# Local attention in a streaming encoder block: 64 queries on their own 128 keys instead of 128 queries on 192 keys

## The chip, the cores and the metric

The kernel runs on one NeuronCore of one Trainium2 chip. The metric is the device time of one execution in microseconds (us). Engines are named as the profile names them: PE is TensorE (PEld its weight loads), DVE is VectorE, ACT is ScalarE, POOL is GpSimd, SP issues the DMAs. Everything is computed in fp32. An ordinary fp32 matrix product stands in the trace as two loads of weights and two MATMUL records (a pair of records per product); a transpose stands as one of each. The large products use fp32r operands that the kernel has split into a high and a low part, three products for one.

## What is computed

One block on 2048 tokens of width 1024: an input projection, a sliding-window attention (the part that the change touches), a pooling branch, a cross-attention into 256 memory tokens, three sigmoid gates, an output product, an MLP of width 4096 and a final norm. The window attention has 8 query heads in 2 groups of 4 that share keys and values (head dimension 64). A query in chunk n (chunks of 64 tokens) sees all keys of chunks n-1 and n, that is 128 keys, with a bias of minus slope times distance and a sink logit per head:

```python
def _window_attention(q, k, v, sinks):
    ...
    qb = q.reshape(b, nc, CHUNK, N_KV_HEADS, Q_PER_KV, HEAD_DIM)
    kb = _chunk_band(k, nc)
    vb = _chunk_band(v, nc)
    scores = jnp.einsum('bnqgrd,bnkgd->bngrqk', qb, kb).astype(jnp.float32) * (HEAD_DIM ** -0.5)
    ...
    scores = scores - slopes * dist[None, :, None, None]
    scores = jnp.where(valid[None, :, None, None], scores, NEG_INF)
    ...
    probs = jax.nn.softmax(jnp.concatenate([scores, sink], axis=-1), axis=-1)[..., :-1]
    out = jnp.einsum('bngrqk,bnkgd->bnqgrd', probs.astype(v.dtype), vb)
```

## The kernel before

The sequence is worked in four blocks of 512 tokens (`NBLK`), one turn of a hardware loop on every engine. A block has these stages in order: input projection (keys, values, queries), four window-attention steps `i` = 0 to 3 of 128 queries each, four memory-attention steps with the first gate and the attention branch's product, merge, output product, MLP, final norm. Weights come in pieces of 1024 by 256: SP loads a piece into one of two `stage` slots, ACT copies the high part to `w_hi` (`hi(n, ...)`), DVE subtracts for `w_lo` (`lo(n)`), PE multiplies (`piece(...)`, two tiles of eight k-steps of three products, L979 to L981). Outputs go through a ring of PSUM banks 0 to 3; the attention uses banks 4 to 7 (`ATT` = 4).

The order on each engine is written out by hand. In one window step `i` PE does, in this order:

- the scores of 128 queries, L1077. A query tile of 128 tokens covers two chunks, so it is multiplied with 192 keys (`WIN_KEYS`). The weights (stationary operand) are one head's 128 queries on 64 partitions, the moving operand is the keys. Heads 0 to 3 sit on partitions 0 to 63, heads 4 to 7 on partitions 64 to 127. A PSUM bank holds 512 columns, so the eight heads' parts are packed by the table `SCORE_PARTS` into three banks: ten products, of 192, 128 or 64 keys. Bank 6 takes parts of both halves, and the semaphore `rest_done` keeps the second half's from starting before the first half's is done.
- `piece(W_U + i, ...)`: 48 large products. Between them, at the fifth and the sixth k-step of the second tile (`probs_across`), the probabilities are transposed: per half of the heads four transposes of keys 0 to 127 and four of keys 128 to 191, L984.
- the value products, L1108 and L1109: per head one product on the first 128 keys and one that adds the last 64 keys, each with 64 weight columns (the head dimension). Even heads write PSUM partitions 0 to 63, odd heads partitions 64 to 127, all in bank 7.

Meanwhile DVE adds the distance bias to the scores (L700, one instruction for each part, slope times `dist`), takes the maximum (L705) and forms the exponent's bias (L706 to L708) for each half `f` of four heads, then sums and reciprocals (L716, L717) and scales the probabilities (L718), then splits the next weight piece (`lo(n + 1)`, L611). ACT splits the next piece (`hi(n + 1)`), does the exponentials per head, copies the transposed probabilities out of PSUM (`pt_a`, `pt_b`) and the value product's result into `y0_hi`; DVE writes `y0_lo` (L724). All of ACT's operations stand at L351. PE waits for DVE before the transposes (`p_rdy`) and for ACT before the value products (`pt_rdy`).

At the start of a block PE transposes the values of 576 tokens in tiles of 128 (`v_tm`, five transposes of `v_pad`), and ACT copies the queries into `q_att`, one head pair for each tile.

Of the kernel before, what the change touches and what calls it, by code (L numbers as in the profile page):

```python
# [31 lines left out]
WIN_KEYS = 3 * CHUNK  # L32
# [24 lines left out]


REST = [[(4 * g + 3, 0, WIN_KEYS, 2, g * 256), (4 * g + 2, P, CHUNK, 2, g * 256 + WIN_KEYS)] for g in range(NKV)]
SCORE_PARTS = REST[0] + [(4 * g + r, 0, WIN_KEYS if r < 2 else P, g, r * WIN_KEYS) for g in range(NKV) for r in range(3)] \  # L60
    + REST[1]

# [23 lines left out]
def build(nc, a, out):  # L86
# [27 lines left out]
    q_att = at("q_att", [P, 4, TB], F32, arena + 16 * KB)  # L114
    resid = at("resid", [P, KT, TB], F32, arena + 16 * KB)
    scores = at("scores", [P, NQ, WIN_KEYS], F32, arena + 32 * KB)
    pt_a = at("pt_a", [P, NQ, P], F32, arena + 38 * KB)
    pt_b = at("pt_b", [HD, NQ, P], F32, arena + 42 * KB)
# [27 lines left out]
    v_tm = sb("v_tm", [P, TT + 1, P])  # L146
    dist0 = sb("dist0", [P, WIN_KEYS])
    dist = sb("dist", [P, WIN_KEYS])
# [4 lines left out]
    half_bg = sb("half_bg", [P, 24])  # L153
    sink = sb("sink", [P, NQ])
# [42 lines left out]
    rest_done = sem("rest_done")  # L197
# [47 lines left out]
    w_upv, w_downv, w_mkv = kp(a["w_up"][0]), kp(a["w_down"][0]), kp(a["w_mem_kv"][0])  # L245
    w_br = [kp(a[n][0]) for n in ("w_branch_attn", "w_branch_pool", "w_branch_mem")]
# [8 lines left out]
    def by_head(t, slot, tile, paired):  # L255


        if paired:
            return t[:, slot, :, tile * P:(tile + 1) * P].rearrange("p k (g c) -> p k g c", g=NKV)
        return t[:, slot, :, :].rearrange("p k (g c) -> p k g c", g=NKV)[:, :, :, tile * HD:(tile + 1) * HD]  # L260

    block = nc.Block()
    with block:
# [3 lines left out]
        def _(sp):  # L267
# [17 lines left out]
            for n in range(PIECES0):  # L285
                load(n % 2, w_mkv[:, :, n * PC:(n + 1) * PC], n - 1 if n >= 2 else None)
                if n == 1:
                    sp.dma_start(x_tm[:], x_rows[:, 0:TT, :]).then_inc(x_ld, 16)
                    sp.dma_start(sink[:], a["attn_sinks"][0:1, :].broadcast_to([P, NQ])).then_inc(const_ld, 16)
                    sp.dma_start(g_fin[:], a["norm_final_g"].rearrange("(o n) -> o n", o=1).broadcast_to([P, D]))\  # L290
                        .then_inc(const_ld, 16)
# [6 lines left out]
            with sp.Fori(0, NBLK) as b:  # L298
# [50 lines left out]
        def _(act):  # L349
# [63 lines left out]
            with act.Fori(0, NBLK) as b:  # L413
# [23 lines left out]
                for t in range(4):  # L437
                    if t == 2:
                        hi(W_U, G_Q + 2)
                    copy(q_att[:, t, :], G_Q + t)  # L440
                copy(v_tm[:, 0:TT, :].rearrange("p t n -> p (t n)"), G_VT)
                copy(v_tm[0:CHUNK, TT, :], G_VT + 1, ring[0:CHUNK, (G_VT + 1) % 4, 0:P])


                for i in range(TT):
# [19 lines left out]
                    if i == 0:  # L465

                        act.wait_ge(stored, b + 1)
                    op(y0_hi[:, :, i * P:(i + 1) * P], ps[:, ATT + 3, :].rearrange("p (t n) -> p t n", n=P),
                       ACT.Copy).then_inc(y_hi_done, 1)
# [130 lines left out]
        def _(dve):  # L600
            v = nc.vector

            def low(slot, value, kt=KT, query=False):
# [12 lines left out]
            v.scalar_tensor_tensor(out=dist[:], in0=dist0[:], scalar=-1.0, in1=dist0[:], op0=ALU.mult, op1=ALU.max)\  # L616
                .then_inc(d, 1)
# [3 lines left out]
            v.reciprocal(inv_cnt[:], inv_cnt[:]).then_inc(fin_done, 1)  # L621

            v.memset(dist[0:CHUNK, 2 * CHUNK:], FAR).then_inc(y_done, 1)
            v.memset(dist[CHUNK:P, 0:CHUNK], FAR).then_inc(d, 1)
            dve.wait_ge(d, 6)
            v.tensor_copy(dist0[:], dist[:]).then_inc(d, 1)
            dve.wait_ge(d, 7)

            v.memset(dist0[0:CHUNK, 0:CHUNK], FAR).then_inc(d, 1)
# [32 lines left out]
            dve.wait_ge(const_ld, 32)  # L662
            v.tensor_scalar(sink8[:], sink[:], 1.0 / ATT_SCALE, None, ALU.mult).then_inc(d, 1)
# [3 lines left out]
            d0 = 15  # L667

            D_BLK = 59
            with dve.Fori(0, NBLK) as b:  # L670
# [20 lines left out]
                for i in range(TT):  # L691
# [3 lines left out]
                    dst_ = dist0 if i == 0 else dist  # L695
# [13 lines left out]
                    if i == 0:  # L709

                        v.tensor_copy(dist0[:], dist[:]).then_inc(d, 1)
                        step[0] += 1
                    for f in range(2):
# [10 lines left out]
                    v.tensor_tensor(y0_lo[:, :, i * P:(i + 1) * P],  # L724
                                    ps[:, ATT + 3, :].rearrange("p (t n) -> p t n", n=P),
                                    y0_hi[:, :, i * P:(i + 1) * P].bitcast(F32), ALU.subtract).then_inc(y_done, 1)
# [166 lines left out]
        def _(pool):  # L893
# [8 lines left out]
            g_.iota(dist0[:], [[-1, WIN_KEYS]], base=CHUNK, channel_multiplier=1,  # L902
# [71 lines left out]
        def _(pe):  # L974
# [50 lines left out]
            with pe.Fori(0, NBLK) as b:  # L1025
# [33 lines left out]
                for t in range(TT):  # L1059
                    last = transpose(ring[:, G_VT % 4, t * P:(t + 1) * P], v_pad[:, t * P:(t + 1) * P])  # L1060
                last.then_inc(tile_done, 1)
                transpose(ring[0:CHUNK, G_VT % 4 + 1, 0:P], v_pad[:, TB:TB + CHUNK]).then_inc(tile_done, 1)

                for i in range(TT):
# [18 lines left out]
                    def probs_across(k):  # L1083
# [181 lines left out]
```

## Time and profile before

| what | value |
|---|---|
| median of 3 runs | 3052.1 us (3051.82 to 3055.05) |
| profiled execution: span | 3050.7 us |
| PE busy | 3000.1 us (98%) |
| DVE busy | 1367.5 us (45%) |
| ACT busy | 982.3 us (32%) |
| POOL busy | 194.1 us (6%) |
| granted TensorE clock, mean | 0.996 of 2.4 GHz |
| HBM traffic | 96 GB/s over the span |

The profiled execution's span is 1.4 us below the median of the runs. Matmul records overlap in the trace: a record lasts longer than the time until the next one starts, so what a group of products costs is read from the starts of what comes first and what comes next, and not from its busy time. Rows of the timeline give the start in us, the duration, the engine, the line, the operation, its operands and shape, how many were merged, and in brackets the idle time before and what ended it.

### The profile page before, as it was taken

The numbers are of one execution on the slowest core, as the hardware profiler recorded it, in microseconds if no ns is written. First come the engines' busy times: TensorE is split into PE (matmuls) and PEld (weight loads), VectorE is DVE, ScalarE is ACT, GpSimd is POOL, SyncE is SP. The second block draws the span as 40 slices with busy tenths as digits, with TensorE's granted clock in tenths as the row PEclk, the third lists the DMA queues.
The fourth block names the chain that finished last, engine by engine and source line by source line (L and its number), as shares of the span: only waits on it lengthen the run. The fifth ranks groups of instructions, "written<-read, shape, count | busy, mean of one in ns | idle before, by whom it ended". The sixth has DMA issues, their size and how long they took to land.

```text
span 3050.7 us, 36914 instructions
## 1 busy us (share of the span) xinstructions
PE 3000.1 (98%) x14045; PEld 2468.1 (81%) x14045; DVE 1367.5 (45%) x1709; ACT 982.3 (32%) x1457; POOL 194.1 (6%) x191
## 2 busy tenths in 40 slices
PE   8999999999999999999999999999999999999998
PEld 7788888888778888888877888888887788888886
DVE  4542354444344335544435424544444532454444
ACT  4442232222344233222234423322223432332223
POOL 0100110000010111000001011100000101100000
PEclk9999999999999999999999999999999999999999
DMA  5122333322312233333231224233322122432322
GB/s 187 35 78 85 118 131 97 97 96 97 98 39 90 90 124 118 97 97 100 93 98 39 83 90 164 84 102 97 97 91 84 51 82 97 160 97 92 98 97 86
DMA packets 290351, 294.06 MB, mean 96 GB/s; under 512 B 9704, under 2 KB 285212, under 8 KB 290204
## 3 DMA queue, kind: packets, MB, share of 16 engines
q1 hardware_dynamic: 287900, 283.71, 28.8%
q0 software_dynamic: 2304, 8.39, 0.7%
q8 instruction: 92, 1.51, 0.2%
q14 instruction: 55, 0.45, 0.0%
HBM read 283.67 MB, written 8.39 MB: 96 GB/s over the span
## 4 chain that ended last, share of the span: by engine, by line
PE 90%; issue 5%; DVE 2%; POOL 1%; ACT 1%; DMA 0%; POOLq 0%; DVEq 0%; ACTq 0%
PE ps L979 28%; PE ps L981 27%; PE ps L980 27%; PE ps L984 2%; PE ps L1108 2%; PE ps L1109 2%; PE ps L1077 1%; POOL sq_sum L957 1%; PE ps L1135 1%; PE ps L1118 1%; ACT sq L351 0%; DVE u_lo L792 0%; DVE scores L700 0%; DVE mx L705 0%; DVE out_tm L883 0%
## 5 line engine op out<-in xcount | busy, mean ns | idle before, releaser
L979 PE MATMUL ps<-h_hi,w_hi 128*128 128x512 f32 x2240 | 884.8, 395 | 12.5 <-issue 12.5
L980 PE MATMUL ps<-h_lo,w_hi 128*128 128x512 f32 x2240 | 874.6, 390 | 0.0
L981 PE MATMUL ps<-h_hi,w_lo 128*128 128x512 f32 x2240 | 874.6, 390 | 0.0
L611 DVE TENSOR_TENSOR w_lo<-stage,w_hi 128x2048 fp32r<-128x2048 f32 (+1 forms) x269 | 559.9, 2081 | 643.2 <-ACT w_hi L351 642.0
L351 ACT ACTIVATE w_hi<-stage 128x2048 fp32r<-128x2048 f32 (+2 forms) x287 | 485.1, 1693 | 525.7 <-PE ps L981 524.5
L979 PE MATMUL ps<-u_hi,w_hi 128*128 128x512 f32 x1280 | 501.5, 392 | 5.5 <-DVE u_lo L792 5.5
L979 PEld LDWEIGHTS ps<-h_hi,w_hi 128*128 128x128 f32 x2240 | 422.1, 188 | 100.6 <-issue 14.2
L981 PE MATMUL ps<-u_hi,w_lo 128*128 128x512 f32 x1280 | 498.8, 390 | 0.0
L980 PE MATMUL ps<-u_lo,w_hi 128*128 128x512 f32 x1280 | 498.4, 389 | 0.0
L981 PEld LDWEIGHTS ps<-h_hi,w_lo 128*128 128x128 f32 x2240 | 421.9, 188 | 88.1
L980 PEld LDWEIGHTS ps<-h_lo,w_hi 128*128 128x128 f32 x2240 | 422.1, 188 | 86.4 <-issue 1.0
L979 PEld LDWEIGHTS ps<-u_hi,w_hi 128*128 128x128 f32 x1280 | 240.4, 188 | 56.9 <-DVE u_lo L792 4.4
L981 PEld LDWEIGHTS ps<-u_hi,w_lo 128*128 128x128 f32 x1280 | 240.3, 188 | 50.2
L980 PEld LDWEIGHTS ps<-u_lo,w_hi 128*128 128x128 f32 x1280 | 240.5, 188 | 48.8
L351 ACT ACTIVATE u_hi<-temp 128x512 fp32r<-128x512 f32 x128 | 80.9, 632 | 512.3 <-DVE temp L836 512.3
L854 DVE TENSOR_TENSOR resid<-resid,ps 128x512 f32<-128x512 f32 x128 | 88.0, 688 | 338.0 <-PE ps L981 338.0
L351 ACT ACTIVATE temp<-ps,half_bg 128x512 f32<-128x512 f32 x96 | 66.1, 689 | 357.8 <-PE ps L981 357.8
L836 DVE SCALAR_TENSOR_TENSOR temp<-ps,inv_rms 128x512 f32<-128x512 f32 x128 | 88.5, 692 | 205.3 <-PE ps L981 204.8
L979 PE MATMUL ps<-y_hi,w_hi 128*128 128x512 f32 x400 | 157.6, 394 | 0.0
L981 PE MATMUL ps<-y_hi,w_lo 128*128 128x512 f32 x400 | 155.9, 390 | 0.0
L980 PE MATMUL ps<-y_lo,w_hi 128*128 128x512 f32 x400 | 155.8, 389 | 0.0
L949 POOL TENSOR_TENSOR resid<-resid,temp 128x512 f32<-128x512 f32 x64 | 83.9, 1321 | 938.0 <-DVE temp L784 938.0
(154 smaller groups left out, 2081.9 us busy)
## 6 DMA issues: line engine op xcount, KB each, us to landing
stage<-in_w_up SPq DMA_DIRECT2D x128, 512.0 KB, 4.6
stage<-in_w_down SPq DMA_DIRECT2D x128, 512.0 KB, 4.0
stage<-in_w_gate SPq DMA_DIRECT2D x96, 512.0 KB, 4.2
stage<-in_w_in SPq DMA_DIRECT2D x60, 512.0 KB, 4.7
stage<-in_w_out SPq DMA_DIRECT2D x32, 512.0 KB, 4.1
x_tm<-in_x SPq DMA_DIRECT2D x5, 2048.0 KB, 9.5
stage<-in_w_branch_attn SPq DMA_DIRECT2D x32, 256.0 KB, 3.0
stage<-in_w_branch_pool SPq DMA_DIRECT2D x32, 256.0 KB, 3.0
```

What stands on the lines that cost most here:

```text
L351: return nc.scalar.activation(*args, **kw)
L611: v.tensor_tensor(w_lo[:, slot, 0:kt, :], stage[:, slot, 0:kt, :], w_hi[:, slot, 0:kt, :].bitcast(F32), ALU.subtract).then_inc(lo_done, 1)
L836: v.scalar_tensor_tensor(out=temp[:, t % 2, :], in0=ring[:, t % 4, :], scalar=0.0, in1=inv_rms[:], op0=ALU.max, op1=ALU.mult)\
L854: v.tensor_tensor(resid[:, 2 * i + z, :], resid[:, 2 * i + z, :], ring[:, t % 4, :], ALU.add).then_inc(emptied[t % 4], 1)
L949: g_.tensor_tensor(dst, dst, temp[:, 2 * g + z, :], ALU.add).then_inc(sum_rdy, 1)
L957: g_.tensor_tensor(sq_sum[:], sq_sum[:], sq[:, m % 2, :], ALU.add).then_inc(sq_add, 1)
L979: mm(dst, wh, xh, start=first, stop=False)
L980: mm(dst, wh, xl, start=False, stop=False)
L981: return mm(dst, wl, xh, start=False, stop=last)
L984: return nc.tensor.transpose(dst, src, ident[0:n, 0:n])
L1108: mm(o, v_tm[:, i, g * HD:(g + 1) * HD], pt_a[:, h, :], start=True, stop=False)
L1109: last = mm(o, v_tm[0:HD, i + 1, g * HD:(g + 1) * HD], pt_b[:, h, :], start=False, stop=True)
```

## The change

A score tile now holds two heads of one chunk (2 by 64 queries) instead of one head of two chunks, and meets only the 128 keys which its chunk may see.

- `q_att` is laid out by chunk, `[P, chunk, pair member, 64]`, so that two heads of a chunk are 128 adjacent columns. A step `i` has eight score products of 128 keys (2 chunks, 2 head pairs, 2 groups), with the groups, and so the partition halves, alternating. Group 0 writes bank 4 and group 1 bank 5 alone; `rest_done` is gone.
- The bias is precomputed for each head pair (`bias`, and `bias0` for the first chunk, whose keys before it are masked by -1e30). DVE adds it with two TENSOR_TENSOR of 256 columns for each half in place of five SCALAR_TENSOR_TENSOR.
- Maximum, exponential and scaling work on 128 instead of 192 columns for each of the eight tiles.
- There is one transpose for each tile (eight in a step, sixteen before), two copies `pt` by ACT (four before).
- The value product takes the transposed probabilities of two tiles, four heads, as one moving operand of 256 columns: four products of 64 weight columns in a step (sixteen before). Group 0 writes PSUM partitions 0 to 63, group 1 partitions 64 to 127.
- `v_tm` holds the 128 keys of each of the eight chunks, overlapping: eight transposes and two copies of 512 columns at a block's start, before five transposes and copies of 512 and 128 columns.
- The channel order of `y0` changes with this, so `w_branch_attn` is loaded to match: two DMAs of 64 partitions by 4 rows, before two of 128 partitions by 2 rows, of the same 128 KB each.
- The sinks are rearranged by four small copies at the start, and the bias tables are built at the start: eight operations of 64 by 128 and a few more. `dist` and `v_tm` move into the shared arena. In step 0 of a block `bias0` is overwritten with `bias`, 512 columns (before `dist0`, 192 columns).

```diff
-WIN_KEYS = 3 * CHUNK
+WIN_KEYS = 2 * CHUNK
+NCH = TB // CHUNK
...
                     load(n % 2, w_gate[:, :, j * PC:(j + 1) * PC], lo0 + n)
-                    load((n + 1) % 2, w_br[0][:, :, j * PC:(j + 1) * PC], lo0 + (n + 1), kt=4)
+                    load((n + 1) % 2, [w_attn[g][:, :, j * PC:(j + 1) * PC] for g in range(NKV)], lo0 + (n + 1),
+                         dst=[stage[g * HD:(g + 1) * HD, (n + 1) % 2, 0:4, :] for g in range(NKV)])
...
-                    copy(q_att[:, t, :], G_Q + t)
-                copy(v_tm[:, 0:TT, :].rearrange("p t n -> p (t n)"), G_VT)
-                copy(v_tm[0:CHUNK, TT, :], G_VT + 1, ring[0:CHUNK, (G_VT + 1) % 4, 0:P])
+                    copy(q_att[:, :, t, :], G_Q + t, ring[:, (G_Q + t) % 4, :].rearrange("p (c n) -> p c n", n=CHUNK))
+                for z in range(2):
+                    copy(v_tm[:, 4 * z:4 * z + 4, :].rearrange("p t n -> p (t n)"), G_VT + z)
...
-                        op(pt_a[:, hs, :].rearrange("p h n -> p (h n)"), ps[:, ATT + f, :], ACT.Copy)
-                        last = op(pt_b[:, hs, :].rearrange("p h n -> p (h n)"), ps[0:HD, ATT + 2 + f, :], ACT.Copy)
+                        last = op(pt[:, hs, :].rearrange("p h n -> p (h n)"), ps[:, ATT + f, :], ACT.Copy)
...
-                        for h, k0, n_, bank, col in SCORE_PARTS:
-                            if h // HALF == f:
-                                last = v.scalar_tensor_tensor(
-                                    out=scores[:, h, k0:k0 + n_], in0=dst_[:, k0:k0 + n_],
-                                    scalar=-SLOPES[h] / ATT_SCALE, in1=ps[:, ATT + bank, col:col + n_],
-                                    op0=ALU.mult, op1=ALU.add)
+                        for c in range(2):
+                            last = v.tensor_tensor(scores[:, f * HALF + 2 * c:f * HALF + 2 * c + 2, :],
+                                                   (bias if c else first)[:, 2 * f:2 * f + 2, :],
+                                                   ps[:, ATT + f, c * 256:(c + 1) * 256].rearrange("p (t n) -> p t n", t=2),
+                                                   ALU.add)
...
-                    for h, k0, n_, bank, col in SCORE_PARTS:
-                        g, t = h // 4, h % 4
-                        if (h, k0, n_, bank, col) == REST[1][0]:
-
-
-                            pe.wait_ge(rest_done, b4 + (i + 1))
-                        last = mm(ps[:, ATT + bank, col:col + n_], q_att[g * HD:(g + 1) * HD, t, i * P:(i + 1) * P],
-                                  k_pad[g * HD:(g + 1) * HD, i * P + k0:i * P + k0 + n_], start=True, stop=True)
-                        if (h, k0, n_, bank, col) == REST[0][1]:
-                            last.then_inc(rest_done, 1)
+                    for c in range(2):
+                        for t in range(2):
+                            for g in range(NKV):
+                                last = mm(ps[:, ATT + g, (2 * c + t) * P:(2 * c + t + 1) * P],
+                                          q_att[g * HD:(g + 1) * HD, 2 * i + c, 2 * t:2 * t + 2, :].rearrange("p t n -> p (t n)"),
+                                          k_pad[g * HD:(g + 1) * HD, (2 * i + c) * CHUNK:(2 * i + c) * CHUNK + P],
+                                          start=True, stop=True)
...
                         for h in range(f * HALF, (f + 1) * HALF):
-                            transpose(ps[:, ATT + h // 4, (h % 4) * P:(h % 4 + 1) * P], scores[:, h, 0:P])
-                        for h in range(f * HALF, (f + 1) * HALF):
-                            last = transpose(ps[0:HD, ATT + 2 + h // 4, (h % 4) * P:(h % 4 + 1) * P],
-                                             scores[:, h, P:])
+                            last = transpose(ps[:, ATT + f, (h % HALF) * P:(h % HALF + 1) * P], scores[:, h, :])
...
-                    for h in range(NQ):
-                        g = h // 4
-                        o = ps[(h % 2) * HD:(h % 2 + 1) * HD, ATT + 3, (h // 2) * P:(h // 2 + 1) * P]
-                        mm(o, v_tm[:, i, g * HD:(g + 1) * HD], pt_a[:, h, :], start=True, stop=False)
-                        last = mm(o, v_tm[0:HD, i + 1, g * HD:(g + 1) * HD], pt_b[:, h, :], start=False, stop=True)
+                    for c in range(2):
+                        for g in range(NKV):
+                            last = mm(ps[g * HD:(g + 1) * HD, ATT + 3, c * 256:(c + 1) * 256],
+                                      v_tm[:, 2 * i + c, g * HD:(g + 1) * HD],
+                                      pt[:, 4 * g + 2 * c:4 * g + 2 * c + 2, :].rearrange("p t n -> p (t n)"),
+                                      start=True, stop=True)
```

On PE, the scores at a block's first step, before; `k_pad` are the keys, `q_att` the queries, shapes are output rows by columns:

```order
L1077 MATMUL ps<-k_pad,q_att 128x192
L1077 MATMUL ps<-k_pad,q_att 128x64
L1077 MATMUL ps<-k_pad,q_att 128x192 x2
L1077 MATMUL ps<-k_pad,q_att 128x128
L1077 MATMUL ps<-k_pad,q_att 128x192 x2
L1077 MATMUL ps<-k_pad,q_att 128x128
L1077 MATMUL ps<-k_pad,q_att 128x192
L1077 MATMUL ps<-k_pad,q_att 128x64
```

and on PE from the first half's transposes of the same step to the next step's scores, now (`pt` are the transposed probabilities, `v_tm` the values):

```order
L998 MATMUL ps<-ident,scores 128x128 x4
L993 MATMUL ps<-h_hi,w_hi 128x512
L994 MATMUL ps<-h_lo,w_hi 128x512
L995 MATMUL ps<-h_hi,w_lo 128x512
...
L1116 MATMUL ps<-pt,v_tm 64x256 x4
L1089 MATMUL ps<-k_pad,q_att 128x128 x8
```

The ten score products of three widths have become eight of 128 columns, and the value products between the last large product and the next scores are four of 256 columns, where before eight rows of L1108 and eight of L1109, in turn and of 128 columns, stood.

On DVE, one half's bias and maximum in the first step, before:

```order
L700 SCALAR_TENSOR_TENSOR scores<-dist_89,ps 128x192
L700 SCALAR_TENSOR_TENSOR scores<-dist_89,ps 128x64
L700 SCALAR_TENSOR_TENSOR scores<-dist_89,ps 128x192 x2
L700 SCALAR_TENSOR_TENSOR scores<-dist_89,ps 128x128
...
L705 TENSOR_REDUCE mx<-scores 128x4
```

and now:

```order
L715 TENSOR_TENSOR scores<-bias_89,ps 128x256
L715 TENSOR_TENSOR scores<-bias,ps 128x256
...
L720 TENSOR_REDUCE mx<-scores 128x4
```

Two additions stand where five multiply-adds stood; nothing else has changed its place on DVE inside the step.

## Rows read from the trace of the kernel before

**Rows 1.** The page: busy time of the engines, and the chain that ended last.

```profile
PE 3000.1 (98%) x14045; PEld 2468.1 (81%) x14045; DVE 1367.5 (45%) x1709; ACT 982.3 (32%) x1457; POOL 194.1 (6%) x191
...
PE 90%; issue 5%; DVE 2%; POOL 1%; ACT 1%; DMA 0%; POOLq 0%; DVEq 0%; ACTq 0%
```

**Rows 2.** Waits of PE: who waited for whom, total us, times, longest.

```profile
PE ps L1077 <- ACT q_att L351: 1.3, 4, 0.3
PE ps L984 <- DVE scores L718: 1.1, 4, 0.3
```

**Rows 3.** Timeline of PE, second block: start us, us, what, xcount, [idle before].

```profile
826.52 0.71 PE L984 MATMUL ps<-ident,v_pad 128*128 128x128 f32 x5
827.57 2.61 PE L1077 MATMUL ps<-k_pad,q_att 64*128 64x192 f32 x20 [0.34 <-ACT q_att L351]
...
830.11 0.50 PE L979 MATMUL ps<-h_hi,w_hi 128*128 128x512 f32 x1
...
838.39 1.03 PE L984 MATMUL ps<-ident,scores 128*128 128x128 f32 x8
...
839.95 1.03 PE L984 MATMUL ps<-ident,scores 128*128 128x128 f32 x8
...
842.98 0.43 PE L1108 MATMUL ps<-pt_a,v_tm 128*64 128x128 f32 x2
843.35 0.43 PE L1109 MATMUL ps<-pt_b,v_tm 64*64 64x128 f32 x2
...
848.76 2.61 PE L1077 MATMUL ps<-k_pad,q_att 64*128 64x192 f32 x20
...
851.30 0.50 PE L979 MATMUL ps<-h_hi,w_hi 128*128 128x512 f32 x1
```

**Rows 4.** Timeline of other fp32 products of the block, PE and its weight loads.

```profile
931.99 1.95 PE L1135 MATMUL ps<-m_pt,mem_v 128*128 128x128 f32 x16
...
912.89 1.59 PEld L1118 LDWEIGHTS ps<-mem_k,q_mem 128*128 128x128 f32 x8 [0.17 <-issue]
```

**Rows 5.** Timeline of score weight loads alive at 828.20, 828.70 and 829.60 us.

```profile
828.11 0.30 PEld L1077 LDWEIGHTS ps<-k_pad,q_att 64*128 64x128 f32 x2
...
828.55 0.35 PEld L1077 LDWEIGHTS ps<-k_pad,q_att 64*128 64x128 f32 x4
...
829.42 0.30 PEld L1077 LDWEIGHTS ps<-k_pad,q_att 64*128 64x128 f32 x2
```

**Rows 6.** Groups of PEld by form: busy us, mean ns, idle before and why.

```profile
L1108 PEld LDWEIGHTS ps<-pt_a,v_tm 128*64 128x64 f32 x256 | 24.5, 134 | 24.8 <-issue 24.8
```

**Rows 7.** Timeline of DVE in a window step.

```profile
830.22 1.21 DVE L700 SCALAR_TENSOR_TENSOR scores<-dist,ps 128x192 f32<-128x192 f32 x5 [9.66 <-PE ps L1077]
831.47 0.95 DVE L705 TENSOR_REDUCE mx<-scores 128x4 f32<-128x768 f32 x1
...
835.64 0.25 DVE L711 COPY dist<-dist 128x192 f32<-128x192 f32 x1
...
838.17 0.96 DVE L718 TENSOR_TENSOR scores<-scores,rd 128x768 f32<-128x768 f32 x1
839.04 2.29 DVE L611 TENSOR_TENSOR w_lo<-stage,w_hi 128x2048 fp32r<-128x2048 f32 x1
849.49 0.69 DVE L724 TENSOR_TENSOR y_lo<-ps,y_hi 128x512 fp32r<-128x512 f32 x1 [8.16 <-ACT y_hi L351]
```

**Rows 8.** Timeline of ACT, a window step's last copy and a branch piece's split.

```profile
841.52 0.58 ACT L351 ACTIVATE pt_b<-ps 64x512 f32<-64x512 f32 x1
...
937.30 1.05 ACT L351 ACTIVATE w_hi<-stage 128x1024 fp32r<-128x1024 f32 x1
```

**Rows 9.** Timeline of SP and DMA issues (KB each, median us to landing), 890 to 930 us.

```profile
927.83 0.88 SPq L283 DMA_DIRECT2D stage<-in_w_branch_attn  x2
...
stage<-in_w_branch_attn SPq DMA_DIRECT2D x2, 256.0 KB, 2.9
```

**Rows 10.** Timeline of DVE at the program's start.

```profile
7.35 0.21 DVE L631 COPY par<-ps 128x52 f32<-128x52 f32 x1 [3.17 <-PE ps L984]
...
40.35 2.29 DVE L611 TENSOR_TENSOR w_lo<-stage,w_hi 128x2048 fp32r<-128x2048 f32 x1 [2.81 <-ACT w_hi L351]
```

More of the change, by code:

```diff
@@ L145, in build @@
     v_pad = sb("v_pad", [P, CHUNK + TB])
-    v_tm = sb("v_tm", [P, TT + 1, P])
-    dist0 = sb("dist0", [P, WIN_KEYS])
-    dist = sb("dist", [P, WIN_KEYS])
+    v_tm = at("v_tm", [P, NCH, P], F32, arena + 42 * KB)
+    dist = at("dist", [P, WIN_KEYS], F32, arena + 40 * KB)
+    bias0 = sb("bias0", [P, 4, WIN_KEYS])
+    bias = sb("bias", [P, 4, WIN_KEYS])
     g_fin = sb("g_fin", [P, D])
@@ L260, in by_head, with y0_tile, by_chunk @@
         return t[:, slot, :, :].rearrange("p k (g c) -> p k g c", g=NKV)[:, :, :, tile * HD:(tile + 1) * HD]
+    def y0_tile(t, i):
+        return t[:, :, i * P:(i + 1) * P].rearrange("p t (c n) -> p c t n", c=2)
+    def by_chunk(bank):
+        return bank.rearrange("p (c t n) -> p c t n", c=2, t=4)
     block = nc.Block()
@@ L467, in _ @@
                         act.wait_ge(stored, b + 1)
-                    op(y0_hi[:, :, i * P:(i + 1) * P], ps[:, ATT + 3, :].rearrange("p (t n) -> p t n", n=P),
-                       ACT.Copy).then_inc(y_hi_done, 1)
+                    op(y0_tile(y0_hi, i), by_chunk(ps[:, ATT + 3, :]), ACT.Copy).then_inc(y_hi_done, 1)
                 for j in range(4):
@@ L621, in _ @@
             v.reciprocal(inv_cnt[:], inv_cnt[:]).then_inc(fin_done, 1)
-            v.memset(dist[0:CHUNK, 2 * CHUNK:], FAR).then_inc(y_done, 1)
-            v.memset(dist[CHUNK:P, 0:CHUNK], FAR).then_inc(d, 1)
+            v.scalar_tensor_tensor(out=bias[:, 0, :], in0=dist[:], scalar=-1.0, in1=dist[:], op0=ALU.mult, op1=ALU.max)\
+                .then_inc(y_done, 1)
+            dve.wait_ge(y_done, 1)
+            v.tensor_copy(dist[:], bias[:, 0, :]).then_inc(d, 1)
             dve.wait_ge(d, 6)
-            v.tensor_copy(dist0[:], dist[:]).then_inc(d, 1)
+            for c in range(4):
+                for r in range(2):
+                    rows_ = slice(r * CHUNK, (r + 1) * CHUNK)
+                    last = v.tensor_scalar(bias[rows_, c, :], dist[rows_, :], -SLOPES[2 * c + r] / ATT_SCALE, None, ALU.mult)
+            last.then_inc(d, 1)
             dve.wait_ge(d, 7)
-            v.memset(dist0[0:CHUNK, 0:CHUNK], FAR).then_inc(d, 1)
+            v.tensor_copy(bias0[:, :, CHUNK:], bias[:, :, CHUNK:])
+            v.memset(bias0[:, :, 0:CHUNK], -FAR).then_inc(d, 1)
             dve.wait_ge(misc_done, 1)
@@ L662, in _ @@
             dve.wait_ge(const_ld, 32)
+            for r in range(2):
+                rows_ = slice(r * CHUNK, (r + 1) * CHUNK)
+                by_pair = sink_h[rows_, :].rearrange("p (g t r) -> p g t r", g=NKV, t=2)[:, :, :, r]
+                for c in range(2):
+                    last = v.tensor_copy(sink[rows_, :].rearrange("p (g c t) -> p g c t", g=NKV, c=2)[:, :, c, :], by_pair)
+            last.then_inc(d, 1)
+            dve.wait_ge(d, 14)
             v.tensor_scalar(sink8[:], sink[:], 1.0 / ATT_SCALE, None, ALU.mult).then_inc(d, 1)
@@ L666, in _ @@
             low(1, 6, query=True)
-            d0 = 15
+            d0 = 16
             D_BLK = 59
@@ L694, in _ @@
                     dve.wait_ge(att_done, att0 + (4 * i + 1))
-                    dst_ = dist0 if i == 0 else dist
+                    first = bias0 if i == 0 else bias
                     for f in range(2):
                         hs = slice(f * HALF, (f + 1) * HALF)
-                        for h, k0, n_, bank, col in SCORE_PARTS:
-                            if h // HALF == f:
-                                last = v.scalar_tensor_tensor(
-                                    out=scores[:, h, k0:k0 + n_], in0=dst_[:, k0:k0 + n_],
-                                    scalar=-SLOPES[h] / ATT_SCALE, in1=ps[:, ATT + bank, col:col + n_],
-                                    op0=ALU.mult, op1=ALU.add)
+                        for c in range(2):
[3 more added lines that the diff above has]
+                                                   ALU.add)
                         chained(last)
@@ L709, in _ @@
                     if i == 0:
-                        v.tensor_copy(dist0[:], dist[:]).then_inc(d, 1)
+                        v.tensor_copy(bias0[:], bias[:]).then_inc(d, 1)
                         step[0] += 1
@@ L1058, in _ @@
                     pe.wait_ge(emptied[G_VT % 4 + z], e0 + G_VT // 4)
[L1059 to L1062, printed above, removed]
+                for z in range(2):
+                    for t in range(4):
+                        c = 4 * z + t
+                        last = transpose(ring[:, G_VT % 4 + z, t * P:(t + 1) * P], v_pad[:, c * CHUNK:c * CHUNK + P])
+                    last.then_inc(tile_done, 1)
                 for i in range(TT):
@@ L1104, in _ @@
                             pe.wait_ge(emptied[G_VT % 4 + z], e0 + (G_VT // 4 + 1))
-                    for h in range(NQ):
-                        g = h // 4
-                        o = ps[(h % 2) * HD:(h % 2 + 1) * HD, ATT + 3, (h // 2) * P:(h // 2 + 1) * P]
-                        mm(o, v_tm[:, i, g * HD:(g + 1) * HD], pt_a[:, h, :], start=True, stop=False)
-                        last = mm(o, v_tm[0:HD, i + 1, g * HD:(g + 1) * HD], pt_b[:, h, :], start=False, stop=True)
+                    for c in range(2):
+                        for g in range(NKV):
[3 more added lines that the diff above has]
+                                      start=True, stop=True)
                     last.then_inc(att_done, 1)
```

23 lines of the change are left out of this document (9 added, 14 removed).

## The prediction

> **What bounds the kernel now.** The page's busy times come first: PE is busy for 98% of the span, and the chain that ended last runs through PE for 90% [rows 1]. So the question is how much PE time the window attention takes, and whether another engine becomes late when PE gets faster. Next come the waits of PE: in all 16 window steps PE lost 1.1 us to late probabilities and, at the four block starts, 1.3 us to late queries [rows 2]. The attention steps are thus PE's own work, and that work is read from starts in PE's timeline [rows 3]. In the second block the scores start at 827.57 and the next large product at 830.11: 2.54 us. The value products start at 842.98, the next scores at 848.76: 5.78 us. Eight transposes last 1.03 us as merged, their last record alone about 0.27, so one follows another after (1.03 - 0.27) / 7 = 0.109 us; sixteen are 1.74 us. A step costs PE 2.54 + 5.78 + 1.74 = 10.06 us beside its large products, and 16 steps 161 us. The clock is at its upper level (2.4 GHz) in these stretches; the page's mean of 0.996 leaves nothing to win there.
>
> **Unit prices.** Sixteen records of 128 columns follow each other after (1.95 - 0.28) / 15 = 0.11 us. The eight weight loads between products of 256 columns follow after (1.59 - 0.19 - 0.11) / 6 = 0.215 us; the 0.11 is the first gap, in which the array has not yet begun [rows 4]. So a record costs 0.11 at 128 columns and 0.215 at 256, two to a product. The ten score products carry 1536 columns, at 0.215 for 256 and two records 2.58 us of streaming alone, and yet they take 2.54 us with their filling and emptying. Part of it overlapped, and the loads show where: at 828.20 and 829.60 two loads are alive, 0.30 us from the first start to the last end; at 828.70 four are alive within 0.35 us, so that three gaps fill 0.35 - 0.19 = 0.16 us, 0.05 each, half of what one product after another allows [rows 5]. That is the place where the products of heads 0 to 3 (partitions 0 to 63) hand over to those of heads 4 to 7. Two partition halves work at the same time. The value products show the contrary: L1108 starts at 842.98, L1109 at 843.35, a step of 0.36 us where two records of 128 columns need 0.22 [rows 3], and the weight load before each stands idle for 24.8 / 128 = 0.19 us [rows 6]. Each of the sixteen products begins only when the one before has left the array. Each also changes between 128 and 64 contracted rows.
>
> **Transposes.** Eight instead of sixteen: 8 x 0.109 = 0.87 us saved a step. At a block's start three are added, 0.33 us. Before, the five start at 826.52, the last ends its streaming some 0.5 us after, and the scores begin only at 827.57, held by the copy of the last queries [rows 3]. The 0.33 fits in these 0.5 us and costs nothing; without that cover it would be 4 x 0.33 = 1.3 us.
>
> **Scores.** Eight products of 128 columns, sixteen records, with the halves alternating and each in its own bank. If both halves run at once, each has eight records: 0.11 to load, 7 x 0.11 to the last start, 0.20 from the last start to the next large product (before, the group ends at 827.57 + 2.61 = 830.18, its last record of 0.27 began at 829.91, the next product at 830.11), together 1.08, and about 0.12 lag of the second half: 1.2 us. If they run one after another: 0.11 + 15 x 0.11 + 0.20 = 2.0 us. I take 1.2, since the trace shows the overlap with the very same operands, and saved are 1.34 us a step.
>
> **Value products.** Four of 64 weight columns and 256 moving columns. All contract 128 rows; nothing changes between them but the half of the output partitions. Lower bound, both halves of columns at once: 0.05 us (half a load) + 0.215 to the second record, 2 x 0.215 to the last start, 0.31 to the next group (0.20 plus the 0.11 by which the record is longer), 1.0, with a lag 1.1 us. In between, one after another without emptying: 0.27 + 6 x 0.215 + 0.31 = 1.9 us. Upper bound, each product waits as today: four times 0.36 + 2 x (0.215 - 0.11) = 0.57, that is 2.3 us. No row shows two column halves with equal rows in a row of products, so all three stay possible. I take 1.1: a mere change of the half did not empty the array where the trace has one [rows 5], and what all the slow products share is the changing number of rows, which is gone. Saved: 5.78 - 1.1 = 4.68 us a step.
>
> Two rules of the Trainium skill bear on this place, and they pull apart. The page "TensorEngine Tiling (Array Packing)", Tiling Modes, Key Properties, says that a change of the tiling mode drains the array, a change of the tile alone does not, and that tiles can load and multiply in parallel; the 0.36 us of rows 3 and the loads of rows 5 agree, and no row shows it for column tiles. The page "TensorE: Matmul & The Clock Gate", Part 3, says that a weight load overlaps a running matmul only where the row group differs; the four value products all use every row. By the first the step costs 1.1 us, by the second near 2.3.
>
> **What lies beside PE.** The chain from scores to probabilities gets shorter. Today DVE starts at 830.22 and ends the second scaling at 838.17 + 0.96 = 839.13, 8.9 us later, with five additions (1.21), a maximum (0.95) and a scaling (0.96) for each half [rows 7]. Two additions of 256 columns are bounded by 2 x 0.69 (512 columns, L724) and 1.21 x 512 / 768 = 0.8; I take 0.8. Maximum and scaling at two thirds of the columns are 0.65 each. A half saves about 0.4 + 0.3 + 0.3, the chain some 2 us after both halves and the smaller exponentials. The overwriting of `bias0` in a block's first step grows from 0.25 to at most 0.25 x 512 / 192 = 0.67. From scores to transposes PE still has its own 8 us of large products (830.11 to 838.39, [rows 3]). One thing comes later: `y0_lo` (0.69 after its wait) must leave DVE before the next scores, and with scores of 1.2 us it ends some 0.2 us after them; the 2 us cover that. So the wait for late probabilities vanishes, 1.1 us in all [rows 2]. ACT's last copy of probabilities ended at 841.52 + 0.58 = 842.10, 0.9 us before the values [rows 8, 3]; the transposes of the second half are now 0.43 us shorter, but so are the copies, one instead of two. DVE's next piece (`lo`, 2.29) ends at 841.33 and is wanted at 851.30; a step shrinks by 7 us, the chain before it by 2, so about 5 us remain. The branch weights come by 64 partitions instead of 128: issued at 927.83, landing 2.9 us later, split at 937.30, that is 6.5 us of cover [rows 8, 9]; even twice the transfer time hides. The start: DVE stands idle 3.17 us before `par`, and the new bias operations (some fifteen, each of 128 columns or fewer by partition, mostly 0.1 to 0.3) fit; the sink copies fall into 2.81 us [rows 10]. These edits cost nothing; uncovered, the start would cost up to 2 us once.
>
> **The sum.** 1.34 + 4.68 + 0.87 = 6.89 us a step, 16 steps 110.2, plus 1.1: 111 us. From the profiled span 3050.7 that leaves 2939.4; the median of the runs lies 1.4 above the span, so I predict **2941 us**.
>
> **Rivals.**
> - Columns one after another: the value products take 1.9, that is 16 x 0.8 = 13 us more, 2954 us. For it: twice the operand stream on the same 128 partitions at once has no row in the trace.
> - Columns emptied at each product: 16 x 1.2 = 19 us more, 2960 us. For it: the sixteen products of today, which also alternate halves. Against: they always change the row number too. This is the second page's rule.
> - Rows one after another: the overlap of rows 5 lasts only over a handover, and alternating might lose it. Scores 2.0, 13 us more: 2954 with fast columns, 2973 with emptied ones.
> - A new wait takes the place: PE arrives at the transposes before the probabilities. For that the DVE chain would have to lose the 2 us that it gains. At 1 us late a step that is 16 us, 2957 us.
> - Slower than before: the same wait, if the new additions and scalings (three-dimensional operands over half-tiles) ran much slower than the rows of the same size. PE gains 6.9 us a step and has about 2 to spare, so the chain must grow by 9 us, from 7 to 16, before the kernel is slower; at 18 us it is 16 x 2 = 32 us over, 3084 us. Nothing in rows 7 points to it.
> - The edit does not do what it says: the two halves of a score tile need no less PE time. Excluded by the count of columns, 1536 to 1024.
>
> **How the numbers follow.** Forecast 50%; columns in turn 18%; columns emptied 14%; rows in turn with any columns 10%; a wait for DVE of up to 2 us a step 5%; slower 2%; more gain than forecast (no lags: 16 x 0.2 = 3 us, 2938) 1%. The range from 2935 to 2962 holds the first three and part of the others. Faster by over 0.2% (what a measurement here can tell from no change) 0.97, within 0.2% 0.01, slower 0.02.
>
> **What would show it.** Right: score group to next large product 1.2 us, values to next scores 1.1, weight loads of scores and of values alive four at a time, no PE wait for the scaling on DVE (L718). Wrong: gaps of 0.2 us before each value load mean emptied columns; record starts spaced 0.215 without gaps mean columns in turn; a PE wait for DVE scores in each step means the chain.

## The result and the profile after

| | before | changed |
|---|---|---|
| median of the runs | 3052.3 us (4 runs) | 2946.24 us (2944.52 to 2946.61, 4 runs) |
| span of the profiled execution | 3050.7 us | 2944.8 us |
| ratio, with its 95% interval | | 0.9647 (0.9634 to 0.9661) |

The forecast was 2941 us in a range from 2935 to 2962. The changed kernel is 106 us faster, 3.5%, where 111 were forecast. The page of the changed kernel opens like that of before [rows 1]: PE is still busy for 98% of a span that is 106 us shorter.

```profile
PE 2890.6 (98%) x13481; PEld 2391.0 (81%) x13481; DVE 1350.5 (46%) x1625; ACT 961.5 (33%) x1425; POOL 195.3 (7%) x191
...
PE 90%; issue 5%; DVE 2%; POOL 1%; ACT 1%; DMA 0%; DVEq 0%; POOLq 0%; ACTq 0%
```

The changed kernel's PE in the second block, transposes of the values, scores, values, as in [rows 3] of before (start, duration, what, count):

```profile
801.06 1.03 PE L998 MATMUL ps<-ident,v_pad 128*128 128x128 f32 x8
802.11 1.16 PE L1089 MATMUL ps<-k_pad,q_att 64*128 64x128 f32 x16
803.20 0.50 PE L993 MATMUL ps<-h_hi,w_hi 128*128 128x512 f32 x1
...
811.54 0.60 PE L998 MATMUL ps<-ident,scores 128*128 128x128 f32 x4
...
815.28 1.08 PE L1116 MATMUL ps<-pt,v_tm 128*64 128x256 f32 x8
816.29 1.16 PE L1089 MATMUL ps<-k_pad,q_att 64*128 64x128 f32 x16
817.38 0.50 PE L993 MATMUL ps<-h_hi,w_hi 128*128 128x512 f32 x1
```

Scores now take 803.20 - 802.11 = 1.09 us (2.54 before) and values 816.29 - 815.28 = 1.01 (5.78 before). A weight load of the scores never comes alone: at 802.50 four are alive within 0.31 us, which before was so only at the handover between the partition halves [rows 5]. The eight loads of the values lie within 0.63 us, where loads 0.215 apart, one product after another, would spread over 6 x 0.215 = 1.3 us at least.

```profile
802.32 0.31 PEld L1089 LDWEIGHTS ps<-k_pad,q_att 64*128 64x128 f32 x4
...
815.28 0.63 PEld L1116 LDWEIGHTS ps<-pt,v_tm 128*64 128x64 f32 x8 [0.35 <-issue]
```

A step from scores to scores is then shown by the windows of the same block, each one step (its length, then busy time and instruction count of PE, PEld, DVE, ACT and POOL, then granted clock as a share of 2.4 GHz, DMA share and GB/s). First the changed kernel's steps 1, 2 and 3:

```profile
816.29:830.43 14.14, 14.14 (x82) 11.17 (x80) 8.57 (x20) 8.16 (x24) 0.14 (x1) 1.00 0.27 89
830.43:846.45 16.02, 14.54 (x82) 11.02 (x80) 13.19 (x20) 8.17 (x24) 11.05 (x10) 1.00 0.05 17
846.45:860.60 14.15, 14.15 (x83) 11.18 (x81) 8.57 (x20) 8.16 (x24) 0.00 (x0) 1.00 0.21 56
```

and steps 1 and 2 of the kernel before:

```profile
848.76:869.97 21.21, 21.21 (x117) 16.10 (x117) 10.66 (x26) 9.55 (x26) 4.59 (x5) 1.00 0.15 50
869.97:891.68 21.71, 21.43 (x117) 15.98 (x116) 11.90 (x26) 9.54 (x26) 6.27 (x6) 1.00 0.08 25
```

A quiet step went from 21.21 to 14.14: 7.07 us saved. Step 2 went from 21.71 to 16.02 only: 5.69. In that window DVE's busy time rises to 13.19 us for the same 20 instructions that take 8.57 in its neighbours, and all ten window sums that POOL does in a block (the pooling branch's, L946) stand there, the first of them beginning 0.14 us earlier. PE now waits for DVE there: one wait of 1.5 us in each block, four in all, where before it was one of 0.3 in each [rows 2]. The first line is from the table of waits, the second is the wait in the second block, before the second half's transposes of step 2.

```profile
PE ps L998 <- DVE scores L733: 5.9, 4, 1.5
...
842.79 0.66 PE L998 MATMUL ps<-ident,scores 128*128 128x128 f32 x4 [1.48 <-DVE scores L733]
```

The row counts idle time from the end of the last record. From start to start the step is longer by more, 16.02 - 14.14 = 1.88 us.

Twelve quiet steps and four steps 2 give 12 x 7.07 + 4 x 5.69 = 107.6 us. The spans differ by 105.9. The remaining 1.7 us lie between the last values of one block and the first scores of the next, and are taken up at the end.

### The profile page after: what moved, and what is told of

It reads as the page before. It is cut to its first block, busy times and chain, and to the rows that moved or that the text cites. A ratio compares the mean times of both kernels' runs of the same rounds, so it can differ in the third digit from the quotient of the medians.

```text
span 2944.8 us, 35670 instructions
## 1 busy us (share of the span) xinstructions
PE 2890.6 (98%) x13481; PEld 2391.0 (81%) x13481; DVE 1350.5 (46%) x1625; ACT 961.5 (33%) x1425; POOL 195.3 (7%) x191
## 4 chain that ended last, share of the span: by engine, by line
PE 90%; issue 5%; DVE 2%; POOL 1%; ACT 1%; DMA 0%; DVEq 0%; POOLq 0%; ACTq 0%
PE ps L993 29%; PE ps L995 28%; PE ps L994 28%; PE ps L998 1%; POOL sq_sum L971 1%; PE ps L1145 1%; PE ps L1128 1%; PE ps L1116 1%; PE ps L1089 0%; ACT sq L357 0%; DVE u_lo L806 0%; DVE scores L733 0%; DVE out_tm L897 0%; DVE scores L715 0%; DVE h_lo L656 0%
```

## Experiments

Five altered kernels ran, and the changed kernel once more; each ratio is to runs of the kernel before on the same chip. The changed kernel's repetition, POOL's spread, the order of the halves and the narrow value products shared one chip. The doses in DVE's chain and the equal rows ran on another, where the changed kernel did not run.

**The changed kernel again.**

> The changed kernel as it is, beside the next three on one chip. Both theories expect 2946 us, within 0.1%.

2945.47 us, ratio 0.9646 (0.9631 to 0.9661). Its step 2 again takes 16.0 us, the others 14.1.

**Spread POOL's work.** The ten sums start when their data are there and DVE's chain is over, not all at once.

```diff
+POOL_AFTER = {0: G_UX, 1: G_UX + 2, 3: G_UX + 4}
...
-                for z in range(4):
-                    pool.wait_ge(emptied[z], e0 + (G_UX // 4 + 1))
...
                 for g in range(GROUPS):
+                    if g in POOL_AFTER:
+                        q = POOL_AFTER[g]
+                        pool.wait_ge(emptied[q % 4], e0 + (q // 4 + 1))
```

> The changed kernel, and only POOL's ten window sums (11.6 us in a block, until now all from the start of window step 2) start elsewhere: group 0 when its tile is copied, groups 1 and 2 from the middle of step 1, group 3 from the middle of step 2, when DVE's chain there is nearly over. Theory (POOL's additions hold up those DVE instructions that read two tiles of SBUF, so that the probabilities of step 2 come late): the four PE waits of 1.5 us for DVE in step 2 vanish, step 2 costs 14.1 us as the others do (16.0 now), 4 x 1.9 = 7.5 us less, 2938.7 us. Rival (step 2 is slow for another reason, its copy targets change from u_pad to q_mem there): step 2 stays at 16.0 and the time at 2946.

2938.78 us, ratio 0.9626 (0.9613 to 0.9639), 6.7 us below the changed kernel on the same chip, of 7.5 expected. Steps 1, 2 and 3 of the block in the same kind of windows:

```profile
814.37:828.51 14.14, 14.14 (x83) 11.17 (x81) 9.44 (x20) 8.18 (x24) 6.08 (x4) 1.00 0.24 79
828.51:842.65 14.14, 14.14 (x83) 11.17 (x81) 9.46 (x20) 8.18 (x24) 7.59 (x6) 1.00 0.20 63
842.65:856.80 14.15, 14.15 (x83) 11.18 (x81) 8.58 (x20) 8.19 (x24) 0.69 (x1) 1.00 0.14 35
```

All steps are 14.14 us, and no wait of PE for the scaled probabilities is left. The theory holds and the rival (the other copy targets in step 2) falls, since these did not change. POOL and DVE still meet, but where nobody waits. The trace of the changed kernel shows how they meet. DVE's chain in step 2:

```profile
834.73 0.74 DVE L715 TENSOR_TENSOR scores<-bias,ps 128x256 f32<-128x256 f32 x2
835.50 0.69 DVE L720 TENSOR_REDUCE mx<-scores 128x4 f32<-128x512 f32 x1
836.23 0.85 DVE L721 TENSOR_TENSOR mx<-mx,sink 128x4 f32<-128x4 f32 x1
837.11 0.17 DVE L722 TENSOR_SCALAR nb<-mx 128x4 f32<-128x4 f32 x1
837.32 0.91 DVE L723 TENSOR_TENSOR sn<-sink,nb 128x4 f32<-128x4 f32 x1
...
838.54 1.35 DVE L733 TENSOR_TENSOR scores<-scores,rd 128x512 f32<-128x512 f32 x1
```

the same instructions in step 1:

```profile
819.14 0.16 DVE L721 TENSOR_TENSOR mx<-mx,sink 128x4 f32<-128x4 f32 x1
...
819.54 0.16 DVE L723 TENSOR_TENSOR sn<-sink,nb 128x4 f32<-128x4 f32 x1
...
822.03 0.69 DVE L733 TENSOR_TENSOR scores<-scores,rd 128x512 f32<-128x512 f32 x1
```

and POOL beside step 2:

```profile
836.00 1.05 POOL L946 TENSOR_TENSOR win_sum<-win_tmp 128x521 f32<-128x521 f32 x1
837.14 1.07 POOL L946 TENSOR_TENSOR win_tmp<-u_pad 128x527 f32<-128x527 f32 x1
838.28 1.06 POOL L946 TENSOR_TENSOR win_sum<-win_tmp 128x525 f32<-128x525 f32 x1
```

An operation on four numbers per partition takes 0.85 or 0.91 us instead of 0.16, and it ends at 837.08 and 838.23, just after POOL's operation that ended at 837.05 and 838.21. The instructions so held are those with two inputs in SBUF. The additions that take one input from PSUM (L715), the reduction (L720) and the one-input L722 keep their times. It works the other way too. With the sums spread, `w_lo` starts while a sum runs and takes 3.16 us (2.28 alone), and the sum after that takes 2.99 us (1.06 alone) and ends 0.9 us after `w_lo`:

```profile
836.33 1.42 POOL L947 TENSOR_TENSOR win_tmp<-u_pad 128x527 f32<-128x527 f32 x1 [6.23 <-ACT q_mem L358]
837.82 2.99 POOL L947 TENSOR_TENSOR win_sum<-win_tmp 128x525 f32<-128x525 f32 x1
...
836.74 3.16 DVE L616 TENSOR_TENSOR w_lo<-stage,w_hi 128x2048 fp32r<-128x2048 f32 x1
```

The Trainium skill states this on the page "SBUF — State Buffer", section "SBUF: two separate sides": GpSimd and VectorE share a pair of ports as an exclusive lock, and a VectorE operation with two SBUF inputs takes it against a GpSimd operation that reads SBUF. The rows agree with both halves of that: the held operations end 0.02 to 0.03 us after POOL's, and those with one input from PSUM keep 0.74 us.

The second half's scaling closes the chain, in step 1 and in step 2:

```profile
823.91 0.69 DVE L733 TENSOR_TENSOR scores<-scores,rd 128x512 f32<-128x512 f32 x1
...
841.07 1.66 DVE L733 TENSOR_TENSOR scores<-scores,rd 128x512 f32<-128x512 f32 x1
```

From the first addition (817.65 and 831.79) to its end the chain takes 6.95 us in step 1 and 10.94 in step 2, 4.0 more. In step 1 the second half's transposes begin at 826.82, 2.2 us after the chain's end. What is over, 4.0 - 2.2 = 1.8 us, is the 1.88 by which step 2 is longer.

**How much DVE's chain can lose.** Needless reductions of 0.69 us in the chain.

```diff
+DOSES = (2, 4, 0, 6)
...
+                    for _ in range(DOSES[i]):
+                        chained(v.tensor_reduce(mx[:, 0:HALF], g_fin[:, 0:512].rearrange("p (h n) -> p h n", h=HALF), AX_X, ALU.max))
```

> The changed kernel with needless reductions of 0.69 us (0.73 with the wait behind each) in DVE's chain between scores and probabilities: 2 in step 0, 4 in step 1, none in step 2, 6 in step 3 of each block. The output is not changed. Theory (the chain has 2 us to spare in every step but step 2): no wait in step 0, about 1.0 us in step 1, about 2.4 us in step 3, 4 x 3.4 = 13.6 us more, 2960 us. Rival (nothing to spare, as the wait in step 2 could be read): 1.5, 2.9 and 4.4 us, 4 x 8.8 = 35 us more, 2981 us.

2952.79 us (two runs), ratio 0.967 (0.9651 to 0.969), 6.5 us above the changed kernel's first median, which is of another chip; the steps of the profile give 4 x (0.10 + 1.55) = 6.6. From the starts of PE's scores, step 0 takes 14.12 us, step 1 14.24, step 2 16.04 and step 3 15.69. In step 3 the wait stands before the first half's transposes:

```profile
859.16 0.66 PE L1001 MATMUL ps<-ident,scores 128*128 128x128 f32 x4 [1.32 <-DVE scores L736]
```

Four doses (4 x 0.73 = 2.92 us) cost 0.10, six (4.38) cost 1.55. Both give the same reserve: 2.8 us. The theory's direction holds; its reserve of 2 us was too small. It was read at the second half of the heads, 2.2 us in step 1. A delay ahead of both halves also uses up the 0.78 us that DVE idles for ACT between the two scalings, which makes 3.0, and the first half's transposes, at 825.70, come 3.0 us after their scaling as well.

**The order of the halves.**

```diff
-                    for c in range(2):
-                        for t in range(2):
-                            for g in range(NKV):
+                    for g in range(NKV):
+                        for c in range(2):
+                            for t in range(2):
                                 last = mm(ps[:, ATT + g, (2 * c + t) * P:(2 * c + t + 1) * P],
...
-                    for c in range(2):
-                        for g in range(NKV):
+                    for g in range(NKV):
+                        for c in range(2):
                             last = mm(ps[g * HD:(g + 1) * HD, ATT + 3, c * 256:(c + 1) * 256],
```

> The changed kernel with the same products in another order: all eight score products of partitions 0 to 63 and then the eight of 64 to 127 (four and four), and the value products by output half too. Theory (the halves run at once only as far as PE looks ahead, a few instructions, so alternating is what brings the overlap): scores 1.6 to 1.9 us instead of 1.09, values 1.45 to 1.85 instead of 1.01, together 15 to 26 us more, 2961 to 2972 us. Rival (PE finds the other half's products wherever they stand in the queue): 1.09 and 1.01 stay, 2946 us.

2953.09 us, ratio 0.9672 (0.9657 to 0.9686), 7.6 us above the changed kernel beside it, half of what the theory asked at least. Values, scores, next large product:

```profile
817.35 1.09 PE L1116 MATMUL ps<-pt,v_tm 128*64 128x256 f32 x8
818.37 1.71 PE L1089 MATMUL ps<-k_pad,q_att 64*128 64x128 f32 x16
820.01 0.50 PE L993 MATMUL ps<-h_hi,w_hi 128*128 128x512 f32 x1
```

Scores took 1.64 us, as expected of the theory; values took 1.02, as expected of the rival. A quiet step is 14.71 us now, 0.57 more, and step 2 is 16.05 as before: there the longer scores fall into the wait for DVE. Twelve steps at 0.57 are 6.8 us. The starts in the block's first scores tell why: records of the scores active in equal stretches of 0.6 us (PE, PEld, clock and DMA),

```profile
803.60:804.20 0.60, 0.53 (x4) 0.54 (x5) 1.00 0.00 0
804.20:804.80 0.60, 0.60 (x11) 0.60 (x10) 1.00 0.00 0
```

one stream until 804.2, two after. At that time the first half had five of its sixteen instructions left in the queue (three records and two loads). The kernel before shows the same count: its second half's first load, at 828.55 in [rows 5], also started with three records and two loads of the first half left. Of the values the first half has only eight instructions in all; the second half began with six of them waiting. So in these kernels PE looked past five or six waiting instructions. Alternating is needed for the scores (0.55 us a step) but not for two value products a half. The theory was right in kind and underestimated the reach.

**Narrow value products.**

```diff
-                        for g in range(NKV):
-                            last = mm(ps[g * HD:(g + 1) * HD, ATT + 3, c * 256:(c + 1) * 256],
-                                      v_tm[:, 2 * i + c, g * HD:(g + 1) * HD],
-                                      pt[:, 4 * g + 2 * c:4 * g + 2 * c + 2, :].rearrange("p t n -> p (t n)"),
-                                      start=True, stop=True)
+                        for t in range(2):
+                            for g in range(NKV):
+                                last = mm(ps[g * HD:(g + 1) * HD, ATT + 3, (2 * c + t) * P:(2 * c + t + 1) * P],
+                                          v_tm[:, 2 * i + c, g * HD:(g + 1) * HD], pt[:, 4 * g + 2 * c + t, :],
+                                          start=True, stop=True)
```

> The changed kernel with eight value products of 128 columns instead of four of 256, halves alternating. Theory (a product costs its columns, and the load of the next weights hides): 0.05 + 8 x 0.11 + 0.2 = 1.1 us a step instead of 1.01, at most 2 us in all, 2946 to 2948 us. Rival (taking four heads in one product is itself a good part of the gain): each of four more products costs its 0.19 us gap as before, 0.8 us a step, 12 us, 2958 us.

2945.69 us, ratio 0.965 (0.9635 to 0.9665): no difference from the changed kernel.

```profile
814.10 1.09 PE L1117 MATMUL ps<-pt,v_tm 128*64 128x128 f32 x16
815.13 1.16 PE L1089 MATMUL ps<-k_pad,q_att 64*128 64x128 f32 x16
```

Eight products of 128 columns take 1.03 us, four of 256 took 1.01. Taking four heads in one product brings nothing by itself; fewer columns and the missing gaps do.

**What made the value products of before slow.**

```diff
-                        last = mm(o, v_tm[0:HD, i + 1, g * HD:(g + 1) * HD], pt_b[:, h, :], start=False, stop=True)
+                        last = mm(o, v_tm[:, i, g * HD:(g + 1) * HD], pt_a[:, h, :], start=False, stop=True)
```

> The kernel before, where the second value product of each head (L1109) takes the first one's operands again, so that all sixteen products of a step contract 128 rows. This leaves out the contribution of the last 64 keys; order, number, width and output halves of the products stay. Theory (what empties the array before each value product is the change between 128 and 64 contracted rows): the products no longer wait 0.19 us each, 16 take 1.8 to 3.8 us instead of 5.78, 32 to 64 us less, 2988 to 3020 us. Rival (the change of the output half empties it): eight of sixteen switches remain, about 4.6 us a step, 3033 us. Second rival (products with 64 weight columns always wait): nothing changes, 3052 us.

2998.45 us, ratio 0.982 (0.9804 to 0.9836), 55.6 us below the kernel before. This kernel leaves out the last 64 keys' part of the values.

```profile
830.23 0.45 PE L1108 MATMUL ps<-pt_a,v_tm 128*64 128x128 f32 x4
...
832.18 1.14 PE L1077 MATMUL ps<-k_pad,q_att 64*128 64x192 f32 x6
```

The sixteen products take 832.18 - 830.23 = 1.95 us instead of 5.78, with the same number, width and output halves. Thirty-two records at 0.11 would be 3.5 us one after another, so the two output halves also run at once. That every second product contracted 64 rows cost 3.83 us a step, 61 us in all, the lost overlap of the output halves included. The time fell by 55.6: step 2 grew a wait here too, its start to start 19.20 against 17.41 of a quiet step (before 21.71 against 21.21), 4 x 1.3 = 5.2 us.

One rival stays. The run removes the change of rows and the 64-row products together, so a product of 64 rows by 64 columns might empty the array whatever stands beside it. Against it speaks that the 128-row products of before took the same 0.36 us until the next start as the 64-row ones (842.98 to 843.35, then to 843.70), and that the 0.20 us in it, from the last record's start to the next product, are also what the scores (64 rows) take to the large product (128 rows). No run settles it.

## Why the prediction was right, step by step

**Bound and unit prices.** Right: PE's own products were the time, and the prices of 0.11 and 0.215 us a record and the 0.20 us to leave the group carried over.

**Transposes.** Right: 0.87 us a step, and the three added at a block's start cost nothing: from the first of them to the scores it is 1.05 us as before. They now end their streaming near 801.9, and the scores begin at 802.11.

**Scores.** Forecast 1.2, measured 1.09 us: the lag of the second half is not 0.12 but nearly nothing. The overlap read from four rows of a handover was the mechanism. The order of the halves is worth 0.55 us of the 1.45 saved. The other 0.90 was not taken apart; the 512 columns fewer, two records each, are 0.86 us by the price of 0.215 for 256.

**Values.** Forecast 1.1 with both output halves at once, measured 1.01. Of the 4.77 us saved a step, the equal number of rows gives 3.83 and the halved number of columns the other 0.94. The choice of 1.1 among three possible values was argued from the row halves of the scores, since no row showed column halves; the equal rows have now shown its reason. The rival of emptied columns fell. With it falls here a rule of the Trainium skill, page "TensorE: Matmul & The Clock Gate", "Part 3: Packing small matmuls — row/col tiling", that a weight load overlaps running matmuls only where the row group differs: all value products use all 128 rows, and eight records of 0.215 us took 1.01 us. The rule of the Trainium skill's page "TensorEngine Tiling (Array Packing)", Key Properties, that a change of the mode drains the array and different tiles work in parallel, agrees with both: 5.78 us became 1.95 when all products had one shape, and the two column halves ran at once.

**What lies beside PE.** Here a step failed: "the 2 us cover that. So the wait for late probabilities vanishes, 1.1 us in all". It grew to 5.9 us of PE waits, and of the signs of being right this one failed ("no PE wait for the scaling on DVE"). The chain itself did get shorter by the forecast 2 us, from 8.9 to 6.95 in a quiet step, but it was costed from a step in which POOL is idle. POOL begins its sums when step 1's last tile is copied. Before, values of 5.78 us and scores of 2.54 followed that copy, and DVE's chain of step 2 began at 872.62, when more than half of POOL's 11.6 us was over.

```profile
865.07 1.06 POOL L932 TENSOR_TENSOR win_sum<-u_pad 128x527 f32<-128x527 f32 x1 [65.45 <-ACT u_pad L351]
...
872.62 1.21 DVE L700 SCALAR_TENSOR_TENSOR scores<-dist,ps 128x192 f32<-128x192 f32 x5 [1.22 <-PE ps L1077]
```

Now the two groups take 2.1 us together, and the chain of step 2 begins 1.5 us after POOL (831.79 against 830.29) and runs beside all the rest of its work.

```profile
830.29 1.06 POOL L946 TENSOR_TENSOR win_sum<-u_pad 128x527 f32<-128x527 f32 x1 [57.99 <-ACT u_pad L357]
...
831.79 0.74 DVE L715 TENSOR_TENSOR scores<-bias,ps 128x256 f32<-128x256 f32 x2
```

The old trace had the sign of it: step 2's wait of 0.3 us in each block, four in all [rows 2], was read as if spread over all steps and not looked up by step. The rival "a new wait takes the place" named the place and the engine, but had it in every step, from a chain that loses its gain; it came in one of four, from POOL. The extra length of step 2, 16.02 - 14.14 = 1.88 against 0.50 before, is 4 x 1.38 = 5.5 us.

**The other edits.** Right: `bias0`'s copy took 0.42 us (at most 0.67 was allowed), the start did not move (the first scores at 77.4 us in both kernels). The branch weights in halves of 64 partitions land after 4.0 us where those of the other two branches, and its own before, land after 3.0, and nobody waits for them.

```profile
stage<-in_w_branch_attn SPq DMA_DIRECT2D x32, 256.0 KB, 4.0
stage<-in_w_branch_pool SPq DMA_DIRECT2D x32, 256.0 KB, 3.0
```

**The sum.** 16 steps at 7.07 instead of 6.89 add 2.9 us of gain; step 2's collision takes 5.5 back, the 1.1 us did not vanish, and 1.7 us went at the turns of the blocks: 110.2 + 2.9 - 5.5 - 1.7 = 105.9 us. That the total came within 5 us of the forecast is in part luck: the lags that were put too high hid half of the collision that was left out.

## What to carry to other kernels

Small products on part of the array were cheap here as a run of one tile shape: keep 64-row and 128-row products apart, and let the halves alternate so that the other half's next load stands within about five instructions. A shortened engine moves others against each other: before costing a wait at nothing, look up in which loop step each existing wait stands, and what POOL does beside DVE then. With the collision moved away the kernel runs at 2938.8 us, the fastest of those measured.

## What the runs showed of the hardware that was not expected

At each turn between blocks PE idles for about 4 us (3.95 to 4.40 in these two kernels), and its granted clock falls. In the changed kernel the first large product starts at 765.61, after 4.40 us of idling for which the profile shows no releaser, and the windows around it (PE busy, granted clock, DMA) read:

```profile
760.00:764.40 4.40, 1.09 (x8) 1.00 0.62 239
764.40:771.20 6.80, 5.59 (x13) 0.50 0.48 167
771.20:775.00 3.80, 3.80 (x18) 0.99 0.84 268
```

6.8 us at the lower level of 1.2 GHz, where the kernel before at the same place had 3.4:

```profile
792.10:795.50 3.40, 3.29 (x8) 0.50 0.22 84
795.50:799.00 3.50, 3.50 (x17) 1.00 0.83 282
```

At the lower level a large record follows the one before after 0.43 us instead of 0.23, so this turn cost the changed kernel about six records more at the slow pace, 1.2 us. Its idle time before the turn was 0.45 us longer as well. Nothing in the change touches that place. From a block's last values to the next block's scores, the three turns are 1.5 us longer, 0.35 longer and 0.1 shorter than before; that is the remainder left open above. How long the low stretch lasts differed between kernels and turns without a pattern that these runs settle: it was 6.8 us at all three turns of the changed kernel and 3.4 at all three with narrow value products, whose turns are the same instructions and took 2.5 us less together. That bounds what a comparison of single profiles can tell here to some 3 us; the medians of four runs are a better guide.
